# A two-layer streaming encoder on one core: six rows of top-k masks by bitwise selection instead of repeated maxima, and the hand-over from gating to attention rearranged

## What is computed

```
proj = xn @ w_in
a_u, a_v, b_q, b_k, b_v, i_q, i_k, i_w = split(proj)

# A: gMLP, 8 groups of 128 channels
sv    = einsum('gts,bnsgc->bntgc', w, layer_norm(gelu(a_v))) + b_s
a_out = gelu(a_u) * sv

# B: per query the 256 keys with the largest index score, then attention over those
score = einsum('bth,bths->bts', iw, relu(i_q . i_k))
score = where(admissible, score, -inf)          # key chunk <= query chunk
vals, sel = top_k(score, 256)
logits = q . k[sel] * 64**-0.5 + rel_bias       # 16 heads
b_out  = softmax(logits) @ v[sel]

mix = concat([a_out, b_out]) @ w_out
```

## Time and profile before

| | us |
|---|---|
| runs: median (lowest to highest) | 2620.8 (2618.99 to 2628.22) |
| the profiled execution: its time | 2619.45 |
| the profiled execution: its span | 2617.6 |
| PE busy | 2432.2 (93%) |
| DVE busy | 1761.4 (67%) |
| POOL busy | 1471.8 (56%) |
| ACT busy | 1189.7 (45%) |
| mean granted clock of TensorE | 0.978 |

### The profile page before, as it was taken

How to read it: one execution, slowest core, us unless ns; L and a number is a source line. 1 busy time by engine, 2 the same in 40 slices (tenths; PEclk the granted TensorE clock), 3 DMA queues, 4 the chain that set the end, 5 groups by cost and what they waited for, 6 DMA issues and landing times.

```text
span 2617.6 us, 34947 instructions
## 1 busy us (share of the span) xinstructions
PE 2432.2 (93%) x11680; PEld 1999.3 (76%) x11680; DVE 1761.4 (67%) x2933; ACT 1189.7 (45%) x2025; POOL 1471.8 (56%) x821
## 2 busy tenths in 40 slices
PE   7899999798898999999999999977989999999997
PEld 6689877577676788888788887866777888878886
DVE  5599999867566477656565687156649565566676
ACT  5443533456556165444443326255546444434331
POOL 2111787544643317887678741446634888587951
PEclk9999999799999999999999999999999999999999
DMA  5480733633343653454754434655463545654343
GB/s 148 65 121 25 153 95 111 209 101 101 110 133 103 221 171 101 145 164 133 243 187 161 145 112 146 149 153 125 109 205 97 149 139 170 207 208 150 119 137 129
DMA packets 323427, 369.62 MB, mean 141 GB/s; under 512 B 13827, under 2 KB 221731, under 8 KB 320981
## 3 DMA queue, kind: packets, MB, share of 16 engines
q1 hardware_dynamic: 313796, 350.38, 45.7%
q10 hardware_dynamic: 9216, 16.78, 2.2%
q0 software_dynamic: 272, 0.62, 0.1%
HBM read 237.18 MB, written 130.55 MB: 140 GB/s over the span
## 4 chain that ended last, share of the span: by engine, by line
PE 66%; issue 14%; DVE 9%; POOL 5%; ACT 4%; DMA 2%; DVEq 1%; SPq 0%; POOLq 0%; ACTq 0%
PE ps L442 63%; POOL attn_out_split L1164 2%; POOL attn_out L1162 2%; PE ps L2528 1%; DVE masks L1994 1%; DVE max L1990 1%; DVE probs_T L2104 1%; DVE logits L2069 1%; DVE masks L1973 1%; POOL attn_out_split L1160 1%; DMA h_operand_raw<-h_operand_scratch 1%; ACT relu_scores L1426 1%; ACT probs_T L1577 1%; POOL attn_out_low L1157 1%; DVE acc L1806 1%
## 5 line engine op out<-in xcount | busy, mean ns | idle before, releaser
L442 PE MATMUL ps<-xn_T,w_split 128*128 128x512 f32 (+1 forms) x2928 | 679.2, 391 | 6.1 <-ACT x_sums L1309 5.5
L442 PEld LDWEIGHTS ps<-xn_T,w_split 128*128 128x128 f32 (+1 forms) x2928 | 548.0, 188 | 124.7 <-issue 4.6
L442 PE MATMUL ps<-w_operand,h_operand 128*128 128x512 f32 x2016 | 464.5, 393 | 10.4 <-DVE acc L2325 6.8
L398 POOL TENSOR_TENSOR w_split<-w_raw,w_split 128x1024 fp32r<-128x1024 f32 x80 | 195.4, 2453 | 479.0 <-ACT w_split L391 478.7
L442 PEld LDWEIGHTS ps<-w_operand,h_operand 128*128 128x128 f32 x2016 | 382.2, 190 | 92.7 <-issue 10.4
L1186 POOL TENSOR_TENSOR w_split<-w_raw,w_split 128x512 fp32r<-128x512 f32 x168 | 241.8, 1450 | 104.9 <-ACT w_split L1669 103.4
L442 PE MATMUL ps<-x_sums_high,w_split 128*128 128x512 f32 x896 | 285.0, 389 | 0.0
L2327 DVE TENSOR_TENSOR acc<-acc,ps 128x512 f32<-128x512 f32 x288 | 185.9, 681 | 129.6 <-PE ps L442 129.1
L1218 POOL TENSOR_TENSOR w_operand<-w_block,w_operand 128x2048 fp32r<-128x2048 f32 x42 | 207.8, 4947 | 111.4 <-ACT w_operand L1689 111.4
L442 PE MATMUL ps<-w_split,hidden 128*128 128x512 f32 x960 | 224.0, 394 | 9.3 <-POOL w_split L398 6.3
L442 PEld LDWEIGHTS ps<-w_split,hidden 128*128 128x128 f32 x960 | 182.0, 190 | 48.6 <-issue 6.7
(11 more groups left out here) (262 smaller groups left out, 4233.0 us busy)
## 6 DMA issues: line engine op xcount, KB each, us to landing
h_operand_raw<-h_operand_scratch SPq DMA_DIRECT2D x42, 1024.0 KB, 5.3
w_raw<-in_w SPq DMA_DIRECT2D x72, 512.0 KB, 8.1
w_block<-in_w SPq DMA_DIRECT2D x48, 512.0 KB, 5.7
q_scratch<-q_split SPq DMA_DIRECT2D x128, 128.0 KB, 2.5
q_tile<-q_scratch ACTq DMA_DIRECT2D x64, 256.0 KB, 2.7
cat_scratch<-attn_out_split SPq DMA_DIRECT2D x128, 128.0 KB, 2.7
w_raw<-in_w_in SPq DMA_DIRECT2D x30, 512.0 KB, 5.0
h_operand_scratch<-h_even SPq DMA_DIRECT2D x14, 1024.0 KB, 4.4
```

What stands on the lines that cost most here:

```text
L398: nc.gpsimd.tensor_tensor(whl[:, n0 % 4, 1, :], wraw[:, n0 % 4, :], whl[:, n0 % 4, 0, :].bitcast(F32), ALU.subtract).then_inc(w_lo, 1)
L442: return nc.tensor.matmul(out_ap, stat, mov, start=start, stop=stop)
```

## The change

It has five parts.

1. **Selection.** The pairs of MAX8 and MATCH_REPLACE8 go. All six rows are searched together for the 256th largest score, one bit of its float32 pattern after another: 32 passes, each with six counts (a TENSOR_SCALAR that compares a whole row with the row's bound, writes a byte flag per column and adds the flags up by its accumulator), one 6-column step that decides the bits (`sel_turn`) and one that sets the next bound (`sel_bound`). Then `select` makes the six masks with six instructions each, ties included. DVE's layer norm step comes behind bit 18, the 14th pass. The flags lie where `bias_lines` lay, so DVE waits for its store (`line_sp`) before the first pass.
2. **Last gates on DVE.** The gates of groups 6 and 7 go from POOL to DVE, behind the selection.
3. **Last gate's split in its own buffer** (`a_out_split_last`), so that it doesn't wait for a store and `mask_bias` doesn't wait for it. The third logits of step 1 wait for that store instead (`ao_spill` on DVE).
4. **Mask and bias of step 0** are added by POOL in group 7, ahead of the last gate's low part; those of step 1 right behind it, ahead of the last weight split.
5. **First query tiles.** SP loads them to `q_tile_first` behind `k_split`, the last three behind the first bias; ACT's four loads go. PE waits for `v_split` only at the first value product. SP also issues the first unit loads when the first half of the gates is stored, without waiting for the last.

```
-        def topk(pair):
-            ... MAX8 / MATCH_REPLACE8, 32 rounds, then the mask
-        topk((7, 2))
-        rstd(rsv, sdv, sqv) ...
-        topk((6, 3))
-        topk((5, 4))
+        picks = (7, 6, 5, 4, 3, 2)
+        def count(k, op, bounds):
+            n = issued[0]
+            dve.wait_ge(tk, max(bounds, n - 1))
+            return tick(nc.vector.tensor_scalar(flag[:, n % 2, 0:(picks[k] + 1) * P], row(picks[k]), bound[:, k:k + 1].bitcast(F32), None,
+                                                op, ALU.add, accum_out=above[:, k:k + 1]))
+        def select(k):
+            dve.wait_ge(tk, issued[0])
+            tick(nc.vector.tensor_scalar(greater, row(b), bound[:, k:k + 1].bitcast(F32), None, ALU.is_gt, ALU.add, accum_out=above[:, k:k + 1]))
+            n = tick(nc.vector.tensor_scalar(equal, row(b), bound[:, k:k + 1].bitcast(F32), None, ALU.is_equal))
+            n = tick(nc.vector.tensor_tensor_scan(row(b), equal, equal, above[:, k:k + 1], ALU.add, ALU.bypass))
+            n = tick(nc.vector.scalar_tensor_tensor(row(b), row(b), float(TOPK), equal, ALU.is_le, ALU.mult))
+            n = tick(nc.vector.tensor_tensor(row(b), row(b), greater, ALU.add))
+            nc.vector.tensor_scalar(row(b), row(b), 0.5, MASKED, ALU.is_lt, ALU.mult).then_inc(mask_ok, 1)
...
+        dve.wait_ge(line_sp, 32)
+        bounds = tick(nc.vector.memset(bound[:], 0))
+        for bit in range(31, -1, -1):
+            for k in range(len(picks)):
+                counted = count(k, ALU.is_ge, bounds)
+            turned = tick(nc.vector.tensor_scalar(turn[:], above[:], float(TOPK), -1.0 if bit == 31 else float(1 << bit), ALU.is_lt, ALU.mult))
+                bounds = tick(nc.vector.scalar_tensor_tensor(bound[:], bound[:], 1 << (bit - 1), turn[:], ALU.bitwise_xor, ALU.bitwise_xor))
+            if bit == 18:
+                normalizer()
+        for k in range(len(picks)):
+            select(k)
+        for g in range(GATES_POOL, GROUPS):                      # GATES_POOL = 6
+            dve.wait_ge(a_free, A_U + 2 * (g + 1))
+            dve.wait_ge(b_free, B_SV + 2 * (g + 1))
+            nc.vector.tensor_tensor(gu[:], svs[:], gu[:], ALU.mult).then_inc(ao_f, 1)
```

```
 SP, last group
                 sp.dma_start(k2[:].bitcast(F32), k2d).then_inc(o_sp[0], 16)
-                sp.dma_start(bias[:, 0:4], toeplitz(1, 0, 4)).then_inc(at_ld0, 16)
+                for b in range(4):
+                    sp.dma_start(q_first[:, b, 1].bitcast(F32), q2d[b]).then_inc(qs_ld[b], 16)
+                    if b == 0:
+                        sp.dma_start(bias[:, 0:4], toeplitz(1, 0, 4)).then_inc(at_ld0, 16)
 POOL, groups
+            if g == GROUPS - 1:
+                pool.wait_ge(at_ld0, 16)
+                pool.wait_ge(ao_sp, 16 * (GROUPS - 1))
+                pool.wait_ge(mask_ok, 2)
+                mask_bias(0)
+            if g < GATES_POOL:
                 nc.gpsimd.tensor_tensor(gu[:], svs[:], gu[:], ALU.mult).then_inc(ao_f, 1)
...
+        mask_bias(1)
         split_lo(pool, T_O0 + 3)
 ACT, before attention
-        for b in range(4):
-            load_q(act, qst, b, b)
 DVE, near(g, j)
+            if g == 1 and j == 2:
+                dve.wait_ge(ao_sp, 16 * GROUPS)
```

More of the change, by code:

```diff
@@ L20 @@
 F32R = mybir.dt.float32r
+U8 = mybir.dt.uint8
+I32 = mybir.dt.int32
 ALU = mybir.AluOpType
@@ L166, in program @@
     nw2 = const("newton2", [P, NB])
-    m8 = const("max8", [P, 2, 8])
+    bound = const("sel_bound", [P, 6], I32)
+    turn = const("sel_turn", [P, 6], I32)
+    above = const("sel_count", [P, 6])
     mx = const("row_min_far", [P, 2, 4])
@@ L438, in program @@
     FIRST = [0, T_F0, T_P1, T_F1]
+    GATES_POOL = 6
     def mm(out_ap, stat, mov, start, stop):
@@ L1045, in gains, with mask_bias @@
             nc.gpsimd.tensor_tensor(vg, vg, sl[:, P:2 * P].unsqueeze(1).to_broadcast([P, NB, P]), ALU.add).then_inc(vl_f, 1)
+        def mask_bias(g):
+            b = g % NB
+            wn = min(2, b + 1) * P
+            end = mask_off(b) + (b + 1) * P
+            m = masks[:, end - wn:end]
+            if g >= 2:
+                pool.wait_ge(l_free, 4 * (g - 1))
+                own_wait(pool)
+            nc.gpsimd.tensor_tensor(mb[:, g % 2, :, 0:wn], bias[:, 4 * (g // NB):4 * (g // NB) + 4, 2 * P - wn:2 * P],
+                                    m.unsqueeze(1).to_broadcast([P, 4, wn]), ALU.add).then_inc(mb_ok, 1)
+            pool.wait_ge(mb_ok, g + 1)
         for m in range(8):
@@ L1106, in pool_program, with pool_attn0 @@
         pool_ffn(pool, LAYERS[1])
[L1108 to L1126 removed]
+    def pool_attn0(pool, mask_bias):
         pool.wait_ge(mask_ok, 8)
@@ L1545, in act_attn0 @@
     def act_attn0(act):
-        for s_ in range(2):
-            act.wait_ge(q_sp[s_], 512)
-        for b in range(4):
-            load_q(act, qst, b, b)
         def exps(g, j):
@@ L1977, in dve_program @@
                 link(nc.vector.memset(masks[0:HD, mask_off(b) + w - HD:mask_off(b) + w], NEG_OUT))
-        tkc = [0]
-        def topk(pair):
-            rows = [masks[:, mask_off(b):mask_off(b) + (b + 1) * P] for b in pair]
-            base = tkc[0]
-            with dve.Fori(0, TOPK // 8 // 4, 1) as i:
-                for r in range(4):
-                    c = base + 4 * r + 16 * i
-                    for e in range(2):
-                        dve.wait_ge(tk, c + e + 1)
-                        own_wait(dve)
-                        nc.vector.max(m8[:, e], rows[e]).then_inc(tk, 1)
-                    for e in range(2):
-                        dve.wait_ge(tk, c + e + 3)
-                        own_wait(dve)
-                        nc.vector.match_replace(rows[e], m8[:, e], rows[e], NEG_SEL).then_inc(tk, 1)
-            tkc[0] += TOPK // 2
-            for e in range(2):
-                dve.wait_ge(tk, 2 + tkc[0])
-                nc.vector.tensor_scalar(rows[e], rows[e], -2.0e38, MASKED, ALU.is_ge, ALU.mult).then_inc(mask_ok, 1)
@@ L2000, in dve_program, with tick, row @@
-        dve.sem_inc(tk, 2)
-        topk((7, 2))
-        dve.wait_ge(ln_sq, 1)
-        rstd(rsv, sdv, sqv)
-        nc.vector.tensor_tensor(nmr[:], negmu[:], rsv[:], ALU.mult).then_inc(ln_nm, 1)
-        topk((6, 3))
-        topk((5, 4))
+        picks = (7, 6, 5, 4, 3, 2)
+        issued = [0]
+        def tick(ins):
+            ins.then_inc(tk, 1)
+            issued[0] += 1
+            return issued[0]
+        def row(b):
+            return masks[:, mask_off(b):mask_off(b) + (b + 1) * P]
@@ new lines, in dve_program @@
+        dve.wait_ge(line_sp, 32)
+        dve.wait_ge(v_ch, chain[0])
+        bounds = tick(nc.vector.memset(bound[:], 0))
+        for bit in range(31, -1, -1):
+            for k in range(len(picks)):
+                counted = count(k, ALU.is_ge, bounds)
+            dve.wait_ge(tk, counted)
+            turned = tick(nc.vector.tensor_scalar(turn[:], above[:], float(TOPK), -1.0 if bit == 31 else float(1 << bit),
+                                                  ALU.is_lt, ALU.mult))
+            dve.wait_ge(tk, turned)
+            if bit:
+                bounds = tick(nc.vector.scalar_tensor_tensor(bound[:], bound[:], 1 << (bit - 1), turn[:], ALU.bitwise_xor, ALU.bitwise_xor))
+            else:
+                bounds = tick(nc.vector.tensor_tensor(bound[:], bound[:], turn[:], ALU.bitwise_xor))
+            if bit == 18:
+                normalizer()
```

57 lines of the change are left out of this document (30 added, 27 removed).

## The result

Before 2,620.8 us (seven executions, 2,618.07 to 2,628.22), the changed kernel **2,630.2 us** (seven, 2,625.91 to 2,634.61). The ratio of the changed kernel to before is 1.0034 with a 95% interval of 1.0020 to 1.0048: 9.4 us slower by the medians, where 2.6 us of gain were forecast, and outside the 2,613 to 2,626 that the forecast's own bounds allowed. The profiled execution took 2,634.61 us (span 2,632.8), the longest of its seven, so single times of it are compared within the stage and not to the end.

The account below looks back on a forecast made before the run. TensorE, busy 93% of the span, was taken as the bound, so only its waits could yield gain. Hand-over 10.9 us gained less 8.3 lost gives 2.6: median 2,618 us, range 2,607 to 2,632.

Parts of the forecast that it names:

- E: End of TensorE's last u projection, 459.65 us in the first profile of before; forecast to move by 8.3 us, to 468.
- If part A ended as before: 10.9 us gained: Hand-over from gates to attention: with E unmoved, DVE's first row of step 2 comes at 479.6 instead of 490.56 us.
- The other engines follow it, and nothing later in attention differs.: Attention after the hand-over: the whole 10.9 us gained at DVE's first row of step 2 carries through.
- The search: DVE's 32 bit passes: start at 174.3 us, 5.4 us a pass alone plus waits for POOL, end near 398.
- Rival 3: DVE's counts take both shared ports and wait for POOL; search ends near 450, 16 us slower, 2,636 us; chance 0.07.
- The masks: DVE's six rows of six mask instructions: 27 us plus 30 us of waits, selection ends near 456 us.
- The push on POOL: Groups 3 to 6: long mask steps delay POOL 11 us, passed on to TensorE; E moves by 8.3 us.
- The gate on DVE: Moving the gate of group 6 from POOL to DVE gives back 1.2 us.
- Rival 1: Masks don't push POOL, so the whole 10.9 us of the hand-over stand: about 2,609 us; chance 0.20.
- Rival 2: Selection ends late on DVE, last gates stand behind it; decides from 464.5 us on, 2,631 us at 475; chance 0.15.
- Rival 4: Hand-over's early loads come no earlier, or the last store holds DVE's logits; costs 3 to 6 us, 2,622; chance 0.08.

Follow-up runs that it names:

- before, again: The unchanged kernel before, profiled a second time: 2,624.9 us.
- row 2 from below, old hand-over: Kernel before with its old selection shortened (row 2 in 16 rounds instead of 32, layer norm steps in the second pair): 2,620.6 us, ratio 1.0002.
- hand-over alone: The full change without its new selection, all gates on POOL: 2,618.8 us, ratio 0.9994.
- selection alone: Kernel before with only the bitwise selection; loads, gates and buffers as before: 2,633.5 us, ratio 1.0045.
- one compare: The full change with each mask made by one compare instead of six instructions, equal scores not handled: 2,621.7 us, ratio 0.9996; profiled again, 2,618.2 us.
- half search: The full change with one compare per mask and the search stopped after 16 of 32 bits, equal scores not handled: 2,619.6 us, ratio 0.9993.
- masks off the ports: The full change with six more counts and one plain compare replacing the five mask instructions behind the count, equal scores not handled: 2,622.5 us, ratio 1.0004.
- from below, three kernels: Old selection, row 2 in 16 rounds, new hand-over: 2,618.6 us; plus last low part before first mask: 2,617.6; plus second unit's loads behind the store: 2,619.2.
- search, unit later: The full change with one compare per mask, last low part before first mask and second unit's loads behind the last store: 2,621.2 us, ratio 0.9994.
- full change, twice: The full change as measured, 2,630.2 us, ratio 1.0034, and the same kernel unchanged, profiled again: 2,627.4 us.
- gates on POOL: The full change with the gates of groups 6 and 7 back on POOL, the last one before the first mask: 2,627.5 us, ratio 1.0026.
- the last low part first: Row 2 from below with the new hand-over, POOL doing the last gate's low part before the first mask: 2,617.6 us, ratio 0.9983.

## Why the forecast was wrong

All profiles together, in us against the first profile of before. The difference tells how much less time than there lies between E and steady attention:

| kernel | E later | attention later | difference |
|---|---|---|---|
| before, again | 7.8 | 3.3 | -4.5 |
| row 2 from below, old hand-over | 3.3 | 0.4 | -2.9 |
| hand-over alone | 0.8 | -1.5 | -2.3 |
| selection alone | 13.7 | 10.6 | -3.1 |
| one compare, twice | 6.6, 2.9 | 0.2, -2.8 | -6.4, -5.7 |
| half search | 3.1 | -3.7 | -6.8 |
| masks off the ports | 7.1 | -0.1 | -7.2 |
| from below, three kernels | 7.0, 6.5, 2.5 | 1.6, -0.6, -3.8 | -5.4, -7.1, -6.3 |
| search, unit later | 3.1 | -2.3 | -5.4 |
| full change, twice | 17.2, 13.9 | 10.2, 7.6 | -7.0, -6.3 |
| gates on POOL | 16.3 | 9.7 | -6.6 |

Two terms of the sum failed. The first is the larger: "If part A ended as before: 10.9 us gained"; 3 to 5 us were there. It failed in three pieces.

1. **The execution it was read from had the earliest E of all.** Over the twelve profiles without the full masks, itself among them, E lies 0 to 7.8 us later than there, 4.2 in the mean. DVE's selection doesn't hang on TensorE's clock and ended at 483 in both profiles of before. In the first, E was early, so the first row of attention (483.32) stood 2.9 us behind its own mask (479.00 and the some 1.4 us of the first of POOL's two). In the second profile E was late (its last u projection ends at 467.43), that mask was done at 486.8 and the row came at 486.94, behind a wait for POOL:

```profile
454.23 13.20 PE L442 MATMUL ps<-xn_T,w_split 128*128 128x512 f32 x48
```

```profile
486.94 0.29 DVE L2084 CUSTOM_DVE_ANT_0 logits<-ps,mask_bias 128x128 f32<-128x128 f32 x1 [3.98 <-POOL mask_bias L1121]
```

There was nothing to gain from an earlier end of the selection there. The old hand-over costs 2.9 to 4.5 us less in the three other profiles that have it than in the one that I took as the rule.
2. **"The other engines follow it, and nothing later in attention differs."** They don't. The first row of step 2 came 10.1 us nearer to E, 0.8 short of the forecast; by 500 us 7.0 were left. The next late things were `unit_tile`, which SP issues right behind the last store and which lands 9.0 us after its issue in the median instead of 3.7, and TensorE's clock. Before, products came close together from 485 on, and the clock was back at 490, just ahead of the first fill products (490.46). Here those began at 498.90 at 1.2 GHz, and the clock was back at 503.
3. What is left is the difference with the new hand-over (-5.4 to -7.2 where DVE wasn't busy to the last) against that with the old (-2.9 to -4.5): 3 us, and 3 to 5 us by the timed kernels.

The second is a term that the sum put at nothing: TensorE's clock in part A. POOL was pushed about as forecast: its fifteen instructions from 402 to 459 us took 9 us more than 2.41 each (forecast 11). But less of it came to TensorE as waiting than forecast, and the clock, which the sum doesn't have, cost more. TensorE's waits for the low part of v are 6.4 to 6.7 us in the four profiles with the full masks and 1.5 to 2.9, 1.9 in the mean, in the other twelve: **4.6 us** more where the forecast had 8.3. Its time at 1.2 GHz from 348 us to E, added up slice by slice, is 33 to 39 us there and 12 to 29, 22 in the mean, in the others: some 14 us more at half the speed, **7 us**. Together they account for the 11 us by which E moved (below). So the forecast's 8.3 us came near by luck: about half of it was there, and a term that it didn't have made up for the rest. That the long waits bring the slow stretches on is the plainest reading (each was followed by one, and with the waits gone the time fell by 8 to 10 us), but no run here has the waits without the stretches.

The other steps, by their own numbers:

- **The search.** Start 175.0 (174.3), end 399.8 (398). The end was right by luck. The pass alone took 5.74 us (5.4), since each count was some 50 ns longer than MAX8 and the start-to-start distance of a count is its own length less some 0.08: 11 us over 32 passes. The waits of the small steps were 30 us in all where the forecast's terms add up to 41. (Its long pass, 5.4 + 1.0 + 1.8, is 8.2 us and not the 8.0 written.) The Trainium skill's sentence (SBUF — State Buffer, "Who interferes with whom") that the accumulating form of `tensor_scalar` doesn't enter the modes that take the shared ports holds: 192 counts, and 42 more in the masks off the ports, steady beside POOL. Rival 3 is out.
- **The masks.** End 463.2 (456). The scan took 1.55 us at 640 columns and 1.02 at 384 where nothing held it up, 2.1 ns a column, the half speed allowed for with 5 us.
- **The push on POOL.** 8.3 us forecast for E. Against the mean E of the profiles without it, the four with it lie 11 us later (13.7, 16.3, 17.2 and 13.9, mean 15.3, less 4.2); in time it is 7.9 to 10 us. That the masks push POOL and POOL holds TensorE up was right; what it is made of is said above. The earlier trace rows were also misread: the five waits stand behind the projections of groups 2 to 5 and 7, not in groups 1 to 4. The same page ("Who interferes with whom") says of a DVE instruction with two SBUF inputs beside one of POOL that reads SBUF, and of the modes with both ports, that whichever engine issues first has the pair for the whole instruction while the other blocks. The 4.07 us of POOL and the 4.35 us of DVE above agree: each is longer than alone, by 1.7 us and some 2.2, less than one instruction of the other engine.
- **The gate on DVE**, 1.2 us given back: nothing measured.
- **Rival 1** (POOL isn't pushed) is out. The two kernels that took the push away measured 2,621.7 and 2,622.5 us, not its 2,609: its price rested on the same 10.9 us.
- **Rival 2** gave 2,631 by a late selection. The time was its, the mechanism not: DVE waited for ACT at both gates (1.00 and 15.98 us).
- **Rival 4** had two parts. The bias was early enough (POOL's first mask started at E + 7.4). The wait for the last store was there, 3.89 us on DVE, but taking it away (the last low part first) gained nothing measurable, since TensorE then waited for `unit_tile`.

With the terms as these runs have them the sum reads: hand-over 3 to 5 us gained, the push 8 to 11 lost (waits and clock), and 0 to 3 more for the search, which is open. That is 3 to 11 lost; 9.4 were measured.

## What to carry to other kernels

Profile the kernel before twice before pricing a hand-over: what one engine's fixed schedule costs depends on where another's clock happened to put it, and here 3 to 4 of 10.9 us were of that kind. Behind each wait that you take away, list the next three arrivals with their landing times, not one. Price a wait of TensorE with the stretch at 1.2 GHz behind it: here the clock cost more than the waiting. And long DVE steps with two SBUF inputs are dear beside a POOL that feeds TensorE: 42 accumulating counts in their place cost nothing that these runs can tell. The fastest kernels here keep the old selection, do the narrowest row from below, and take the new hand-over: 0.9982 of before.

## What the runs showed of the hardware

- With each wait of TensorE of 2.4 to 4.7 us for POOL went 7 to 10 us at 1.2 GHz, behind it or from its last microsecond or so on (six of six); with waits of 0.5 us in some executions and not in others of one program. The Trainium skill (TensorE: Matmul & The Clock Gate, "What's actually happening") says that "the default state is throttled, and activity releases the throttle"; the direction agrees. That a wait as short as 0.5 us can be followed by 3 to 7 us at half the clock, which is 1.5 to 3.5 us of E, is what I hadn't expected.
- Four loads of 256 KB took SP 2.02 us to issue when the last store had landed, and 4.5 to 5.9 us when they were issued right behind it; their median time to landing went from 3.7 to 7.5 to 9.7 us.
